# Output projection, norms and four feed-forward tiles in two column halves; three gate tiles first in the merge

## The chip, the cores and the metric

One core of a Trainium2 chip runs the whole program. The metric is the device time of one execution in microseconds (us); lower is better. The engines are named PE (TensorE, matrix products), ACT (ScalarE), DVE (VectorE), POOL (GpSimd) and SP (SyncE, which issues the transfers).

## The reference

One layer of a hybrid encoder for 512 prompt positions and 32 sample positions. What matters here comes after the two mixer branches (a Mamba-2 branch `y_ssm` and an attention branch `y_att`):

```python
merged = g_ssm * (y_ssm @ p['w_ssm_out']) + g_att * (y_att @ p['w_att_out'])
x = x + g1 * rmsnorm(merged @ p['w_out'], p['norm_mix_post'])
hn = rmsnorm(x, p['norm_ffn_pre']) * (1 + sc2) + sh2
gate, up = jnp.split(hn @ p['w_ffn_in'], 2, axis=-1)
gate, ffn_new = causal_dwconv(gate, ffn_ctx, p['ffn_conv_w'], p['ffn_conv_b'])
f = (jax.nn.silu(gate) * up) @ p['w_ffn_out']
x = x + g2 * rmsnorm(f, p['norm_ffn_post'])
```

The gates are sigmoids of columns of the input projection. Before `y_ssm` is multiplied, it is normalised in eight groups of 256 channels. D_MODEL is 1024, D_FF is 2816; all data are fp32.

## The kernel before

Activations lie with channels on the 128 partitions and positions in the columns: 512 prompt positions, a gap of 4 and 32 sample positions, TW = 548 columns, in two halves of HW = 274. A weight tile is 1024 input channels by 128 output channels, eight blocks of 128 x 128. For exactness each operand is split into a rounded part and a rest (`hi`, `lo`), and a product takes three matmuls per block and half: 48 matmuls of 274 columns for a tile. The result of a tile needs both halves, so two banks of PSUM, a "slot"; there are four slots.

**The weight stream** (class `Stream`). SP loads tile n into one of three raw buffers; ACT rounds it (`split_hi`), POOL subtracts (`split_lo`), PE multiplies (`multiply`) and counts `used`. There are two buffers for split weights, so `split_hi(n)` waits until tile n-2 is used up. The order of all waits and instructions is written out by hand for each engine, and each engine works strictly through its own list.

**The merge** (first block after the scan). PE computes the tile of the last gate, eight attention tiles (`w_att`), and then, for each of eight output tiles, a gate tile and two tiles of `w_ssm`: 33 tiles. Beside the attention tiles, the eight y groups are normalised: `load_y(g)` into one of `Y_SLOTS = 4` buffers `yl`, ACT's `square`, DVE's `add_squares`, PE's `sum_squares` (a product with ones), ACT's `y_root`, DVE's reciprocal and scaling, ACT's `y_hi` and POOL's `y_lo`. `load_y(g)` for g of 4 and more waits until `y_lo(g-4)` is done with the buffer. DVE's `gated(m)` evicts attention tile m; PE waits for `gated(m-2)` before it starts tile m. Attention data come in eight pieces through four buffers `al`. Before, ACT's round m of these runs as follows, and POOL's loop is the same in both kernels:

```python
for m in range(GROUPS + 1):          # ACT
    if m + 1 < GROUPS:
        square(m + 1)
        y_root(m + 1)
    if m >= 1:
        y_hi(m - 1)
    if m < GROUPS:
        w.split_hi(act, A0 + m + 2)
for m in range(GROUPS + 1):          # POOL
    w.split_lo(pool, A0 + m + 2)
    if m >= 1:
        y_lo(m - 1)
```

**Output projection and norms** (second block). Eight tiles of `w_out` over both halves; ACT copies each out of PSUM and squares it, DVE adds the squares, and after the last tile PE sums them over the channels. Then come the root, the reciprocal, the residual (DVE, eight tiles), the squares of the new x, root and reciprocal, the modulation (DVE), rounding (ACT) and rest (POOL). PE meanwhile makes four rows of the modulation vectors (`modulation_step`, `turn_rows`) and then the first feed-forward tile, block by block as `hq_lo` comes.

**Feed-forward** (third and fourth block). 44 tiles of `w_ffn_in`, in pairs gate and up, and 22 tiles of `w_ffn_out` in eight output tiles; the last norm ends the kernel. All blocks end with all engines waiting for one another.

Of the kernel before, what the change touches and what calls it, by code (L numbers as in the profile page):

```python
# [78 lines left out]
def build_layer(nc, i, o, scratch):  # L79
# [9 lines left out]
    with top:  # L89
# [21 lines left out]
        class Stream:  # L111
# [4 lines left out]
            def __init__(self, stack, tag, sources, base, ready, following):  # L116
# [5 lines left out]
                self.block = 0  # L122

# [3 lines left out]
            def hl_slot(self, n):  # L127
                return (self.base + n) % HL_SLOTS
# [19 lines left out]
            def split_hi(self, act, n):  # L148
# [4 lines left out]
                if n >= HL_SLOTS:  # L153
                    act.wait_ge(self.used, n - HL_SLOTS + 1)  # L154
# [17 lines left out]
            def multiply(self, pe, out, hi, lo, first, last, done=None):  # L172
# [1232 lines left out]
        with ExitStack() as st:  # L1405

            G1, A0 = 0, 1
# [9 lines left out]
            w = Stream(st, "m", src, NCH + GROUPS * GT + 1, True, [])  # L1417
            tmp = [sb(st, f"tmp{n}", [P, TW]) for n in range(3)]
# [7 lines left out]
            with ExitStack() as ms:  # L1426
# [14 lines left out]
                def sum_slot(g):  # L1441
                    return slot(3 - g % 2)

                with nc.Block(no_gpsimd_drain=True) as block:
                    @block.sync
                    def _(sp):
                        def load_y(g):
                            sp.dma_start(flat(yl[g % Y_SLOTS]), scratch["y"][g * P:(g + 1) * P, :]).then_inc(in_y[g % Y_SLOTS], 16)

                        load_y(0)  # L1450
                        for t in range(KB):
                            if t >= 4:
                                sp.wait_ge(alo_s, t - 3)
                            sp.dma_start(al[t % 4], scratch["att"][:, t, :]).then_inc(in_att[t % 4], 16)
                            if t == 3:
                                load_y(1)
                                sp.dma_start(snorm[:], i["ssm_norm"]).then_inc(in_c, 16)
                                w.load(sp, RAW_SLOTS)
                                load_y(2)
                        w.load(sp, RAW_SLOTS + 1)  # L1460
                        sp.wait_ge(alo_s, KB)
                        load_y(3)
                        w.load(sp, RAW_SLOTS + 2)
# [9 lines left out]
                    def _(pool):  # L1473
# [16 lines left out]
                    def _(act):  # L1490
# [17 lines left out]

                        w.split_hi(act, A0)
                        square(0)  # L1510
                        for t in range(KB):
# [15 lines left out]
                        for n in range(23):  # L1527
                            w.split_hi(act, N1 + n + 2)
                            if n % 3 == 0:
                                act.wait_ge(w.used, N1 + n + 1)  # L1530
                                act.wait_ge(m_s, KB + n // 3)
                                act.activation(halves(th[:]), slot(2), ACT.Tanh, scale=0.5).then_inc(th_s, 1)
# [8 lines left out]
                    def _(dve):  # L1541
# [8 lines left out]
                        def gated(m):  # L1550
# [4 lines left out]
                            dve.scalar_tensor_tensor(out=halves(mrg[:, m, :]), in0=halves(mrg[:, m, :]), scalar=1.0, in1=slot(m % 2),  # L1555
                                                     op0=ALU.add, op1=ALU.mult).then_inc(m_s, 1)

                        add_squares(0)
                        for t in range(KB):
                            dve.wait_ge(ahi_s, t + 1)  # L1560
                            dve.tensor_tensor(hq_lo[:, t, :], al[t % 4], hq_hi[:, t, :].bitcast(F32), ALU.subtract).then_inc(alo_s, 1)
                        dve.wait_ge(in_c, 16)
                        for m in range(KB):
                            if m >= 1:
                                gated(m - 1)
                            if m + 1 < GROUPS:
                                add_squares(m + 1)
                            dve.wait_ge(root_s, m + 1)
                            dve.reciprocal(rs[:, m % 2, :], rs[:, m % 2, :]).then_inc(rec_s, 1)
                            dve.wait_ge(rec_s, m + 1)  # L1570
# [619 lines left out]
```

## Time and profile before

| | us |
|---|---|
| median of 3 runs | 1434.98 |
| lowest, highest | 1433.67, 1438.44 |
| the profiled execution | 1436.78 |
| its span, first to last instruction | 1435.0 |

All numbers of the profile belong to the profiled execution. PE is the engine that works longest; its mean granted clock over the span was 0.959 of full speed. A matmul's end is modelled, so the distance between starts tells what one costs, and a busy PE may still be a slow one.

### The profile page before, as it was taken

Reading aid. Unit: us, or ns where it says so; the run is one execution under the profiler, and the core shown is the slowest. Engines: PE = TensorE matmul, PEld = TensorE weight load, DVE = VectorE, ACT = ScalarE, POOL = GpSimd, SP = SyncE. Lnnn points to the kernel's source line nnn. Section 1 sums busy time; section 2 is a strip of 40 time slices with the busy share of each in tenths; the row PEclk is TensorE's granted clock in tenths of the full one; section 3 lists DMA queues with packets and bytes.
Section 4 is the critical chain, followed back from the end, with each engine's and each line's share of the span. In section 5 each row is a group of like instructions: output and inputs, shape, how many; then the busy total and the mean of one; then the engine's idle time right before and its main releaser. Section 6 shows DMA issues by size and latency. Waiting matters only on the chain. (4 is left out here: it accounts for less than half of the span.)

```text
span 1435.0 us, 24802 instructions
## 1 busy us (share of the span) xinstructions
PE 1339.5 (93%) x10265; PEld 1255.5 (87%) x10265; DVE 809.9 (56%) x1288; ACT 508.1 (35%) x879; POOL 530.9 (37%) x315
## 2 busy tenths in 40 slices
PE   4699998999999999998798999988999999999996
PEld 1489988899899999998788999974899999999996
DVE  1745316898898898894780000337466666660105
ACT  2212425455455455453441222332332233332221
POOL 0533322332332333332464443332344444443443
PEclk8699989999999999999899999998799999999998
DMA  8275414433433433334331222541222222222221
GB/s 364 99 265 134 122 53 140 126 95 117 138 102 117 129 112 116 117 100 170 101 106 59 88 89 89 205 187 40 75 89 89 88 84 83 87 90 88 82 81 63
DMA packets 74015, 164.31 MB, mean 115 GB/s; under 512 B 28240, under 2 KB 42352, under 8 KB 70432
## 3 DMA queue, kind: packets, MB, share of 16 engines
q1 hardware_dynamic: 73904, 162.74, 35.2%
q8 instruction: 81, 1.33, 0.4%
q14 instruction: 30, 0.25, 0.1%
HBM read 147.10 MB, written 16.07 MB: 114 GB/s over the span
## 5 line engine op out<-in xcount | busy, mean ns | idle before, releaser
L161 POOL TENSOR_TENSOR w_lo<-raw_w,w_hi 128x1024 fp32r<-128x1024 f32 x174 | 429.0, 2466 | 730.3 <-ACT w_hi L155 730.3
L183 PE MATMUL psum<-hp_hi,w_hi 128*128 128x274 f32 x1472 | 449.8, 306 | 22.4 <-POOL hp_lo L284 13.4
L183 PE MATMUL psum<-hp_lo,w_hi 128*128 128x274 f32 x1472 | 430.9, 293 | 0.0
L183 PE MATMUL psum<-hp_hi,w_lo 128*128 128x274 f32 x1472 | 430.2, 292 | 0.0
L155 ACT ACTIVATE w_hi<-raw_w 128x1024 fp32r<-128x1024 f32 x174 | 184.1, 1058 | 547.0 <-PE psum L183 502.1
L183 PEld LDWEIGHTS psum<-hp_hi,w_hi 128*128 128x128 f32 x1472 | 281.7, 191 | 36.5 <-POOL hp_lo L284 16.1
L183 PEld LDWEIGHTS psum<-hp_lo,w_hi 128*128 128x128 f32 x1472 | 284.5, 193 | 1.3
L183 PEld LDWEIGHTS psum<-hp_hi,w_lo 128*128 128x128 f32 x1472 | 282.7, 192 | 0.0
L183 PE MATMUL psum<-hq_hi,w_hi 128*128 128x274 f32 x832 | 248.7, 299 | 12.5 <-POOL hq_lo L1677 8.5
L183 PE MATMUL psum<-hq_hi,w_lo 128*128 128x274 f32 x832 | 245.5, 295 | 0.0
L183 PE MATMUL psum<-hq_lo,w_hi 128*128 128x274 f32 x832 | 244.2, 294 | 0.0
L183 PEld LDWEIGHTS psum<-hq_hi,w_hi 128*128 128x128 f32 x832 | 161.3, 194 | 16.3 <-POOL hq_lo L1677 11.6
L183 PEld LDWEIGHTS psum<-hq_lo,w_hi 128*128 128x128 f32 x832 | 162.4, 195 | 0.4
L183 PEld LDWEIGHTS psum<-hq_hi,w_lo 128*128 128x128 f32 x832 | 160.8, 193 | 0.0
L1096 DVE SCALAR_TENSOR_TENSOR cv<-raw,gp_all,cv 128x548 f32<-128x548 f32 x96 | 93.1, 976 | 14.2 <-ACT cv L978 12.2
L183 PE MATMUL psum<-y_hi,w_hi 128*128 128x274 f32 x256 | 75.4, 295 | 6.2 <-POOL y_lo L1477 6.2
L1588 DVE SCALAR_TENSOR_TENSOR tmp<-th,psum 128x548 f32<-128x548 f32 x8 | 5.8, 723 | 126.2 <-PE psum L183 126.2
L183 PE MATMUL psum<-y_lo,w_hi 128*128 128x274 f32 x256 | 75.1, 293 | 0.0
L183 PE MATMUL psum<-y_hi,w_lo 128*128 128x274 f32 x256 | 75.0, 293 | 0.0
L1891 DVE COPY fr<-fpar 128x2 f32<-128x2 f32 x22 | 41.2, 1874 | 58.9 <-ACT fr L1866 58.9
L1902 DVE SCALAR_TENSOR_TENSOR fs<-th,tmp 128x548 f32<-128x548 f32 x22 | 53.0, 2408 | 32.1 <-ACT th L1873 32.1
L1123 DVE TENSOR_SCALAR dec<-acs_b,tok_all 128x128 f32<-128x128 f32 (+1 forms) x160 | 66.1, 473 | 8.4 <-PE psum L1272 8.4
(263 smaller groups left out, 2033.0 us busy)
## 6 DMA issues: line engine op xcount, KB each, us to landing
raw_w<-in_w_grp SPq DMA_DIRECT2D x58, 512.0 KB, 3.8
raw_w<-in_w_ffn_in SPq DMA_DIRECT2D x44, 512.0 KB, 3.6
ada<-in_w_ada SPq DMA_DIRECT2D x12, 1024.0 KB, 20.6
raw_w<-in_w_ffn_out SPq DMA_DIRECT2D x22, 512.0 KB, 3.5
acs_b<-mem_acs SPq DMA_DIRECT2D x8, 1096.0 KB, 5.6
raw_w<-in_w_ssm SPq DMA_DIRECT2D x16, 512.0 KB, 3.5
ada_o<-in_w_ada SPq DMA_DIRECT2D x4, 2048.0 KB, 11.3
raw_w<-in_w_qkv SPq DMA_DIRECT2D x13, 512.0 KB, 4.9
```

The lines of the kernel that those rows point to most:

```text
L155: act.activation(flat(w_hi[self.hl_slot(n)]), raw_w[self.raw_slot(n)][:], ACT.Copy).then_inc(self.hi_done, 1)
L161: eng.tensor_tensor(flat(w_lo[self.hl_slot(n)]), raw_w[self.raw_slot(n)][:], flat(w_hi[self.hl_slot(n)]).bitcast(F32), ALU.subtract).then_ ...
L183: mm = pe.matmul(out[:, h, :], w, x[:, cols], start=first and j == 0, stop=last and j == 2)
L1096: ins = dve.scalar_tensor_tensor(out=cv[:, t, :], in0=raw[:, t, 1 + k:1 + k + TW], scalar=par(g, GP_W + 4 * t + k, GP_W + 4 * t + k + 1), ...
L1123: ins = dve.tensor_scalar(dec[u % 2][0:L, r, 0:L], acs_b[0:L, r, c0:c0 + L], tok_all[0:L, g, c, 2, r:r + 1], 0.0, ALU.add, ALU.min)
L1588: link(dve, dve.scalar_tensor_tensor(out=halves(tmp[0][:]), in0=halves(th[:]), scalar=1.0, in1=slot(m % 2), op0=ALU.add, op1=ALU.mult))
L1891: link(dve, dve.tensor_copy(r[:, LEAD + S0 - 2:LEAD + S0], fpar[:, f, 4:6]))
L1902: dve.scalar_tensor_tensor(out=sl[f % 2][:], in0=th[:], scalar=1.0, in1=c[:], op0=ALU.add, op1=ALU.mult).then_inc(fsl_s, 1)
```

## The change

**Merge.** Three gate tiles (the last, the first and the second) come ahead of the attention tiles, and so each SSM pair is followed by the gate tile of two pairs on. The attention data are loaded through four other buffers, and the roundings, squares and roots are put into a new order: in ACT's loop the squares of group m+3 and the root of group m+2 now belong to round m. POOL takes two of the attention rests.

**Two halves.** The output projection runs first over the left half of the columns for all eight weight tiles, then over the right half. The split weights stay on chip for that: to the two buffers come six more (`w.plan` says which tile goes where, `w.wait_free` what it must wait for; `half` multiplies one half). While PE works on the right half, the other engines take the left half through both norms; then PE takes the left half of the first four feed-forward tiles, while the right half goes through the norms, and last the right half of those tiles. The modulation rows are spread between the tiles; that of the last gate is turned only in the last block (`turn_s`).

**Feed-forward.** It starts at tile 4. Weights take turns in four buffers instead of two (`split_ahead`), and the extra pair for the very last weight goes.

The stream: what a split waits for, and the product of one half.

```diff
-if n >= HL_SLOTS:
+if n in self.wait_free:
+    sem, count = self.wait_free[n]
+    if count:
+        act.wait_ge(sem, count)
+elif n >= HL_SLOTS:
     act.wait_ge(self.used, n - HL_SLOTS + 1)
...
+def half(self, pe, out, n, k, hi, lo, h, done=None):
+    if k == 0:
+        self.wait_split(pe, n)
+    wh, wl = w_hi[self.hl_slot(n)][:, k, :], w_lo[self.hl_slot(n)][:, k, :]
+    for j, (w, x) in enumerate(((wh, hi), (wh, lo), (wl, hi))):
+        mm = pe.matmul(out, w, x[:, k, h * HW:(h + 1) * HW], start=k == 0 and j == 0, stop=k == KB - 1 and j == 2)
+    if k == KB - 1 and done is not None:
         mm.then_inc(done, 1)
```

The order of the merge's tiles, and the plan of the split weights (`first` and `second` are the two old buffers).

```diff
-src = [i["w_gate"][8 + KB - 1]] + [i["w_att"][m] for m in range(KB)]
+src = [i["w_gate"][8 + KB - 1], i["w_gate"][0], i["w_gate"][1]] + [i["w_att"][m] for m in range(KB)]
 for m in range(KB):
-    src += [i["w_gate"][m], i["w_ssm"][2 * m], i["w_ssm"][2 * m + 1]]
+    src += [i["w_ssm"][2 * m], i["w_ssm"][2 * m + 1]]
+    if m + 2 < KB:
+        src.append(i["w_gate"][m + 2])
...
+SECOND_PASS = (2, 3, 4, 5, 0, 1, 6, 7)
+w.plan.update({O0: first, O0 + 1: second, O0 + 6: 2, O0 + 7: 3})
+for n in range(4):
+    w.plan[O0 + 2 + n] = w.plan[F0 + n] = 4 + n
+for n in range(F0 + 4, END):
+    w.plan[n] = (first, second, 2, 3)[(n - F0) % 4]
+    w.wait_free[n] = (w.used, n - 3)
+for n in range(2, KB):
+    w.wait_free[O0 + n] = (None, 0)
+for n in range(KB):
+    w.wait_free[F0 + n] = (free_s, n + 1)
```

ACT in the merge.

```diff
+w.split_hi(act, 1)
+square(0)
+att_hi(0)
+act.wait_ge(w.used, G1 + 1)
+act.activation(halves(mrg[:, KB - 1, :]), slot(0), ACT.Tanh, scale=0.5).then_inc(ev_s, 1)
+w.split_hi(act, 2)
+y_root(0)
+square(1)
+for t in range(1, 4):
+    att_hi(t)
 w.split_hi(act, A0)
-square(0)
-for t in range(KB):
-    if t == KB - 2:
-        act.wait_ge(w.used, G1 + 1)
-        act.activation(halves(mrg[:, KB - 1, :]), slot(2), ACT.Tanh, scale=0.5).then_inc(ev_s, 1)
-    act.wait_ge(in_att[t % 4], 16 * (t // 4 + 1))
-    act.activation(hq_hi[:, t, :], al[t % 4], ACT.Copy).then_inc(ahi_s, 1)
+gate_tanh(0, 1, slot(1))
+att_hi(4)
+att_hi(5)
 w.split_hi(act, A0 + 1)
-y_root(0)
+gate_tanh(1, 2, slot(0))
+att_hi(6)
+att_hi(7)
+y_root(1)
+square(2)
 for m in range(GROUPS + 1):
-    if m + 1 < GROUPS:
-        square(m + 1)
-        y_root(m + 1)
     if m >= 1:
         y_hi(m - 1)
     if m < GROUPS:
         w.split_hi(act, A0 + m + 2)
-for n in range(23):
+    if m + 2 < GROUPS:
+        y_root(m + 2)
+    if m + 3 < GROUPS:
+        square(m + 3)
+for n in range(21):
     w.split_hi(act, N1 + n + 2)
```

DVE in the merge, its second part.

```diff
+att_lo(6)
+att_lo(7)
+y_reciprocal(1)
+y_norm(1)
+add_squares(2)
+add_squares(3)
+for g in range(2, GROUPS):
+    y_reciprocal(g)
+    if g + 2 < GROUPS:
+        add_squares(g + 2)
+    gated(g - 2)
+    y_norm(g)
+gated(KB - 2)
 gated(KB - 1)
```

PE in the merge: gate tiles and attention tiles; then the SSM tiles and the first two half tiles of the output projection.

```diff
+tile(0, hp_hi, hp_lo)
+tile(1, hp_hi, hp_lo, 0, 2)
+pe.wait_ge(ev_s, 1)
+tile(0, hp_hi, hp_lo, 1, 4)
 for m in range(KB):
-    if m >= 2:
+    if m < 2:
+        pe.wait_ge(th_s, m + 1)
+    else:
         pe.wait_ge(m_s, m - 1)
     for k in range(KB):
         if m == 0:
-            pe.wait_ge(alo_s, k + 1)
-        w.multiply(pe, slot(m % 2), hq_hi[:, k, :], hq_lo[:, k, :], k == 0, k == KB - 1)
-        if k == 4 and m + 1 < GROUPS:
-            sum_squares(m + 1)
-pe.wait_ge(root_s, GROUPS)
+            wait_att_lo(pe, k)
+        w.multiply(pe, att_slot(m), hq_hi[:, k, :], hq_lo[:, k, :], k == 0, k == KB - 1)
+        if k == 3 and m + 2 < GROUPS:
+            sum_squares(m + 2)
 for m in range(KB):
...
-tile(m % 2, wide_hi, wide_lo, 0, 16)
-tile(m % 2, wide_hi, wide_lo, 8, 16)
...
+    for k in range(16):
+        if m == 0:
+            pe.wait_ge(ylo_s, k + 1)
+        w.multiply(pe, slot(m % 2), wide_hi[:, k, :], wide_lo[:, k, :], k == 0, k == 15)
+    if m + 2 < KB:
+        if m == 0:
+            pe.wait_ge(root_s, GROUPS)
+        else:
+            pe.wait_ge(th_s, m + 2)
+        tile(2, hp_hi, hp_lo)
 for k in range(KB):
     pe.wait_ge(mlo_s, k + 1)
-    w.multiply(pe, slot(0), hp_hi[:, k, :], hp_lo[:, k, :], k == 0, k == KB - 1)
...
+    w.half(pe, psum[:, 0, 0:HW], O0, k, hp_hi, hp_lo, 0, w.used)
+for k in range(KB):
+    w.half(pe, psum[:, 2, 0:HW], O0 + 1, k, hp_hi, hp_lo, 0, w.used)
```

ACT's eviction of a half tile of the output projection; c counts the left half's eight tiles, then the right half's.

```diff
+def out_tile(c):
+    h, j = divmod(c, KB)
+    t = SECOND_PASS[j] if h else j
+    bank = 2 * (j % 2) + h
+    if h:
+        act.wait_ge(free_s, j + 1)
+    else:
+        act.wait_ge(w.used, O0 + j + 1)
+    if c >= 2:
+        act.wait_ge(add_s, 7 * h + j - 2 if j >= 3 else 7 * h + 1 if j == 2 else 6 + j)
+    act.activation(sqo[c % 2], psum[:, bank, 0:HW], ACT.Square).then_inc(sqo_s, 1)
+    act.activation(half_of(mrg[:, t, :], h), psum[:, bank, 0:HW], ACT.Copy).then_inc(ev_s, 1)
```

ACT's order from the end of the left half on.

```diff
+row(0)
+out_root(0)
+w.split_hi(act, F0)
+out_tile(8)
+square(0)
+square(1)
+w.split_hi(act, F0 + 1)
+out_tile(9)
+square(2)
+square(3)
+square(4)
...
+w.split_hi(act, F0 + 2)
+out_tile(10)
+square(5)
+square(6)
+square(7)
+w.split_hi(act, F0 + 3)
+x_root(0)
+out_tile(11)
+h_hi(0)
+h_hi(1)
+out_tile(12)
+h_hi(2)
+h_hi(3)
+h_hi(4)
+out_tile(13)
+h_hi(5)
+h_hi(6)
+h_hi(7)
+out_tile(14)
+w.split_hi(act, F0 + 4)
+out_tile(15)
+out_root(1)
+w.split_hi(act, F0 + 5)
+for c in range(8, 12):
+    square(c)
```

PE in the second block: both passes of the output projection.

```diff
+for m in range(2, KB):
+    pe.wait_ge(ev_s, m - 1)
     for k in range(KB):
...
+        w.half(pe, psum[:, 2 * (m % 2), 0:HW], O0 + m, k, hp_hi, hp_lo, 0, w.used)
+    if m >= 6:
+        row_steps(m - 6)
+mid = {0: (3, lambda: out_squares(0)), 2: (3, lambda: x_squares(1)), 3: (3, lambda: x_squares(4)),
+       4: (3, lambda: x_squares(7))}
+for j, m in enumerate(SECOND_PASS):
+    if j >= 2:
+        pe.wait_ge(ev_s, KB + j - 1)
+    for k in range(KB):
+        w.half(pe, psum[:, 2 * (j % 2) + 1, 0:HW], O0 + m, k, hp_hi, hp_lo, 1, free_s)
+        if j in mid and mid[j][0] == k:
+            mid[j][1]()
+    if j < 2:
+        row_steps(2 + j)
+    if j == 1:
+        x_squares(0)
+    elif j == 2:
+        pe.wait_ge(ev_s, KB)
+        for a in range(2):
+            pe.wait_ge(row_s, a + 1)
+            mm = turn_rows(pe, 0, 8 * a, mod_row[:, a, :])
+        mm.then_inc(turn_s, 1)
+        x_squares(2)
+        x_squares(3)
+    elif j == 3:
+        x_squares(5)
+        x_squares(6)
```

PE in the second block: four feed-forward tiles, left halves, then right halves.

```diff
+for n in range(4):
+    for k in range(KB):
+        if n == 0:
+            pe.wait_ge(hlo_s, k + 1)
+        w.half(pe, psum[:, ffn_bank(n), 0:HW], F0 + n, k, hq_hi, hq_lo, 0)
+        if n == 0 and k == 4:
+            out_squares(1)
+    if n == 1:
+        pe.wait_ge(ev_s, 2 * KB)
+        row_steps(4)
+        row_steps(5)
+        x_squares(8)
+        x_squares(9)
+    elif n == 2:
+        for c in range(10, 16):
+            x_squares(c)
+        row_steps(6)
+        row_steps(7)
+pe.wait_ge(row_s, 4)
 for k in range(KB):
...
+    pe.wait_ge(hlo_s, KB + k + 1)
+    for n in range(3):
+        w.half(pe, psum[:, ffn_bank(n) + 1, 0:HW], F0 + n, k, hq_hi, hq_lo, 1, w.used)
 for k in range(KB):
...
+    w.half(pe, psum[:, ffn_bank(3) + 1, 0:HW], F0 + 3, k, hq_hi, hq_lo, 1, w.used)
+w.block = (F0 + 4) * KB
```

Splits ahead in the feed-forward block; n counts its tiles.

```diff
+def split_ahead(split, eng, n):
+    if n < 2:
+        split(eng, F0 + 6 + n)
+    elif n >= 5:
+        split(eng, F0 + n + 3)
```

Left out are the SP order, the declarations and DVE's order in the second block: sums of the left half's squares (`add_out`), reciprocal, the left half's eight `residual`, reciprocal and eight `modulated`, with the right half's `add_out` put in between as its tiles come, and then the same for the right half. `residual` and `modulated` are the operations of before on one half.

## Rows read from the trace of the kernel before

**Rows 1.** The page, part 1: PE's busy time, share of span, instructions.

```profile
PE 1339.5 (93%) x10265; PEld 1255.5 (87%) x10265; DVE 809.9 (56%) x1288; ACT 508.1 (35%) x879; POOL 530.9 (37%) x315
```

**Rows 2.** Busy time by stretch (windows): stretch, length, engines' busy us, PEclk, DMA.

```profile
667.96:763.75 95.79, 75.11 (x513) 71.22 (x513) 63.12 (x48) 43.46 (x55) 50.91 (x27) 0.92 0.41 136
763.75:906.43 142.68, 142.68 (x1105) 142.68 (x1105) 14.32 (x18) 30.80 (x36) 54.47 (x22) 0.98 0.25 78
906.43:957.40 50.97, 49.47 (x386) 48.82 (x384) 16.25 (x13) 17.38 (x23) 19.80 (x8) 1.00 0.67 265
957.40:1017.83 60.43, 45.36 (x180) 26.32 (x181) 39.68 (x55) 17.57 (x26) 14.96 (x11) 0.75 0.09 24
1017.83:1038.00 20.17, 20.17 (x146) 20.17 (x147) 10.37 (x12) 6.71 (x8) 8.02 (x7) 0.91 0.41 129
```

**Rows 3.** Timeline of PE in the merge: start, us, instruction [idle before <-releaser].

```profile
688.03 2.19 PE L1610 MATMUL psum<-tmp,ones 128*128 128x274 f32 x4 [5.40 <-DVE tmp L1548]
...
698.35 1.19 PE L1610 MATMUL psum<-tmp,ones 128*128 128x274 f32 x4 [0.43 <-DVE tmp L1548]
...
699.51 0.29 PE L183 MATMUL psum<-hq_lo,w_hi 128*128 128x274 f32 x1
...
763.75 0.60 PE L183 MATMUL psum<-y_hi,w_hi 128*128 128x274 f32 x1 [6.21 <-POOL y_lo L1477]
```

**Rows 4.** Timeline of ACT in the merge.

```profile
681.45 0.61 ACT L1514 ACTIVATE mrg<-psum 128x548 f32<-128x548 f32 x1
...
684.12 1.28 ACT L1501 ACT_TABLE_LOAD   x1
685.41 0.72 ACT L1501 ACTIVATE y_rstd<-psum,consts 128x548 f32<-128x548 f32 x1
...
701.92 1.06 ACT L155 ACTIVATE w_hi<-raw_w 128x1024 fp32r<-128x1024 f32 x1 [0.52 <-PE psum L183]
...
712.41 1.12 ACT L1495 ACTIVATE ysq<-yl 128x1096 f32<-128x1096 f32 x1 [1.56 <-DMA yl<-mem_y]
```

**Rows 5.** Timeline of POOL ahead of the first SSM tile.

```profile
758.76 2.34 POOL L161 TENSOR_TENSOR w_lo<-raw_w,w_hi 128x1024 fp32r<-128x1024 f32 x1 [1.05 <-ACT w_hi L155]
761.06 2.63 POOL L1477 TENSOR_TENSOR y_lo<-yl,y_hi 128x548 fp32r<-128x548 f32 x2
```

**Rows 6.** Transfers in the merge: engine, count, KB each, median us to landing.

```profile
yl<-mem_y SPq DMA_DIRECT2D x8, 548.0 KB, 3.6
```

**Rows 7.** Timeline of DVE in the merge.

```profile
706.09 3.56 DVE L1569 RECIPROCAL y_rstd<-y_rstd 128x548 f32<-128x548 f32 x1
709.69 1.49 DVE L1573 SCALAR_TENSOR_TENSOR yl<-yl,snorm,y_rstd 128x548 f32<-128x548 f32 x2
711.10 0.72 DVE L1555 SCALAR_TENSOR_TENSOR mrg<-mrg,psum 128x548 f32<-128x548 f32 x1
713.57 1.78 DVE L1548 TENSOR_TENSOR tmp<-ysq 128x548 f32<-128x548 f32 x1 [1.75 <-ACT ysq L1495]
```

**Rows 8.** Timeline of PE at the output projection's first tile and block end.

```profile
912.98 0.39 PE L183 MATMUL psum<-hp_hi,w_hi 128*128 128x274 f32 x1 [1.05 <-DVE hp_lo L1579]
...
914.45 0.36 PE L183 MATMUL psum<-hp_hi,w_hi 128*128 128x274 f32 x1 [0.45 <-PEq L1444]
```

**Rows 9.** Timeline of PE: turning two rows, then steps of two rows.

```profile
985.85 1.84 PE L210 MATMUL psum<-pick_rows,mod_row_o 128*128 128x2 f32 x16
987.62 3.64 PE L203 MATMUL psum<-ada_o,c_silu 128*32 128x512 f32 x32
```

**Rows 10.** Timeline of DVE in the norms: residual tiles, then modulation tiles.

```profile
974.06 0.72 DVE L1734 TENSOR_TENSOR mrg<-mrg,ors 128x548 f32<-128x548 f32 x1
...
975.65 0.72 DVE L1734 TENSOR_TENSOR mrg<-mrg,ors 128x548 f32<-128x548 f32 x1
...
999.80 0.71 DVE L1751 TENSOR_TENSOR tmp<-mrg,ors 128x548 f32<-128x548 f32 x1
...
1002.25 0.72 DVE L1751 TENSOR_TENSOR tmp<-mrg,ors 128x548 f32<-128x548 f32 x1
```

More of the change, by code:

```diff
@@ L1562, in _, with att_lo @@
[L1562 to L1574 removed]
+                        def att_lo(t):
+                            dve.wait_ge(ahi_s, t + 1)
+                            dve.tensor_tensor(hq_lo[:, t, :], al[t], hq_hi[:, t, :].bitcast(F32), ALU.subtract).then_inc(alo_s, 1)
@@ L1691, in _ @@
-                        for n in range(KB):
-                            if n < KB - 1:
-                                w.split_hi(act, O0 + n + 2)
-                            act.wait_ge(w.used, O0 + n + 1)
-                            act.activation(halves(mrg[:, n, :]), slot(n % 2), ACT.Copy).then_inc(ev_s, 1)
-                            act.wait_ge(ev_s, n + 1)
-                            square(n, n)
-                        w.split_hi(act, F0 + 1)
-                        act.wait_ge(ss_s, 1)
@@ new lines, in _ @@
+                        for m in range(KB):
+                            if m + 2 < KB:
+                                w.split_hi(act, O0 + m + 2)
+                            out_tile(m)
+                        row(0)
[7 more added lines that the diff above has]
+                        square(2)
@@ L1718, in _ @@
                         row(2)
+                        for c in range(12, 16):
+                            square(c)
+                        x_root(1)
                         row(3)
+                        for c in range(8, 16):
+                            h_hi(c)
                     @block.vector
@@ L1744, in _ @@
+                        for c in range(1, KB):
+                            add_out(c)
+                        reciprocal(1, O_BANK[0], 0)
+                        for t in range(3):
+                            residual(t)
+                        add_out(9)
+                        for t in range(3, 6):
+                            residual(t)
+                        add_out(10)
+                        residual(6)
+                        residual(7)
                         dve.wait_ge(turn_s, 1)
-                        link(dve, add_bias(dve, 4 * KB, KB, 6))
+                        link(dve, add_bias(dve, 4 * KB, KB, 0))
@@ new lines, in _ @@
+                        add_out(12)
+                        modulated(5)
+                        modulated(6)
+                        modulated(7)
+                        add_out(13)
+                        add_out(14)
+                        add_out(15)
+                        reciprocal(3, O_BANK[1], 1)
+                        for c in range(8, 16):
+                            residual(c)
+                        reciprocal(4, X_BANK[1], 1)
+                        for c in range(8, 16):
+                            modulated(c)
@@ L1761, in _ @@
                     @block.tensor
                     def _(pe):
-                        def squares(src, s, first, last):
-                            for hh in range(2):
-                                mm = pe.matmul(psum[:, 2 * s + hh, 0:HW], ones[:], src[:, hh * HW:(hh + 1) * HW],
-                                               start=first, stop=last)
-                            mm.then_inc(ss_s, 1)
-                        for m in range(1, KB):
-                            if m >= 2:
-                                pe.wait_ge(ev_s, m - 1)
-                            for k in range(KB):
-                                w.multiply(pe, slot(m % 2), hp_hi[:, k, :], hp_lo[:, k, :], k == 0, k == KB - 1)
@@ L1792, in _, with sums @@
-                        pe.wait_ge(ev_s, KB)
-                        for k in range(KB):
-                            block_step(0, k)
-                        for t in range(KB):
-                            block_step(1, t)
-                            pe.wait_ge(sq_s, KB + t + 1)
-                            squares(sq[t % 2], 2, t == 0, t == KB - 1)
-                        pe.wait_ge(root_s, 1)
-                        turn(0, 6)
-                        for a in (2, 3):
-                            for k in range(KB):
-                                block_step(a, k)
+                        def sums(bank, src, first, last):
+                            return pe.matmul(psum[:, bank, 0:HW], ones[:], src, start=first, stop=last)
```

405 lines of the change are left out of this document (248 added, 157 removed).

## The prediction

> **What bounds the kernel now.** I read the page first: TensorE (PE) is busy for 93% of the span [rows 1], so only time in which PE stands still or runs at a lower granted clock can be won. Then the stretches around the change [rows 2]. The second one, 763.75 to 906.43, holds 23 weight tiles (eight SSM pairs, seven gate tiles) at a granted clock of 0.98; less the 2.9 us that the missing 2% is worth this is 139.8/23 = **6.08 us a tile** at full clock (the upper of the two levels, 2.4 GHz), 3.04 for half the columns. The first stretch holds 10 tiles (60.8 us) in 95.79 us, so the start of the merge loses some 35 us less the sums. The fourth, where the norms sit, holds a single tile in 60.43 us, at a clock of 0.75. The change works on these two.
>
> PE's own timeline in the merge [rows 3] shows three things. Sums of squares for one group cost 1.03 us (698.35 to 699.51, less one 0.13 us matmul). Small waits for DVE stand in front of them. And at 763.75 PE waits 6.21 us for `y_lo`. The reader should look at that one closely: in POOL's queue [rows 5] `y_lo` of the last group stands behind a weight split (`w_lo`), which waits for ACT's `split_hi`, which waits until PE has finished a tile. From the tile's end to `y_lo` done it takes 6.2 us, however early the y data were ready.
>
> **The change part by part.** The sum is made against the profiled execution, 1436.78 us around a span of 1435.0, 0.13% above the median.
>
> *Merge.* The work is the same: 33 tiles (200.6) and eight sums (8.2), 208.8 us. Before, the merge lasted from 667.96 to 906.43, 238.5 us, so 29.7 are waits and clock. After:
>
> (a) Three gate tiles come first (18.2 us, two sums in them) and cover the attention loads and the first reciprocal: the 5.40 us wait [rows 3] goes. At attention tile 0, step 3, the new order wants the sums of group 2. They stand behind, from the end of the third gate tile: ACT's split 1.06, tanh 0.61, two roundings of 0.6, table load 1.28, root 0.72 [rows 4]; DVE's reciprocal 3.56, two scalings 1.49, one add (0.72 like its neighbour of that width, 1.78 beside POOL) [rows 7]: 10.9 us with hops, while PE arrives after 3.04. Wait 7.9. At tile 1 split, root, square and add take 3.7 to 4.7 us against 3.04: 0.9.
>
> (b) The squares of group m+3 are now taken in ACT's round m; before it was group m+1. There are four `yl` buffers, so from group 4 on the load needs `y_lo` of group m-1, and POOL does that in the same round m, behind the split for attention tile m+2 that waits for the end of tile m. That is the queue of rows 5, moved from one place to four (m = 1 to 4). ACT stands at the square until the load is there; DVE stands at `add_squares(m+3)`, and behind it in DVE's queue is `gated(m-1)`, which PE awaits before attention tile m+1. Nothing else is issued to PE in between. The price: 6.21 to `y_lo` [rows 3, 5], load 3.6 [rows 6], square 1.12 [rows 4], add 0.72, `gated` 0.72 [rows 7], hops 0.2: **12.6 us, four times: 50.4**. Lower bound 12.3 (no hops, the load at its median); upper 15 (add 1.78, and the load slowed by the next weight behind it, 1.4).
>
> (c) The 6.21 us wait before the first SSM tile goes: its y parts are awaited one by one. In its place `gated(7)` (0.85) and the last `y_lo`, again behind a split (0.8): 1.6.
>
> (d) Clock: the 6.21 us wait left PE at half clock afterwards, worth the 2.9 us above. Five waits of 7.9 to 12.6 us at 2.7 each: 13.5. Below: 1.0 each, if it recovers sooner.
>
> Merge after: 208.8 + 7.9 + 0.9 + 50.4 + 1.6 + 13.5 = 283.1; **+44.6 us**.
>
> *Output projection to the fourth feed-forward tile.* Before: 906.43 to 1038.00, 131.6 us [rows 2]. After, from the same start:
> - First half tile: step 7 needs the last `hp_lo`, which came at 912.98 [rows 8], 6.55 us after the first matmul; a half tile gets there in 2.7, so the wait grows from 1.05 to 3.9. Then 27 matmuls, 3.4, and 1.5 for clock: 11.5.
> - The next weight's split can begin only in the new block: barrier 0.6 (0.45 idle beyond a modelled end [rows 8]), split 1.06 + 2.34 [rows 4, 5]: 4.1. Before, full tiles gave it cover.
> - Six half tiles 18.2, two row steps (3.64/4 = 0.9 each [rows 9]), clock 2.7, weights late behind the modulation blocks 1: 23.7.
> - Second pass: eight half tiles 24.3, two row steps 1.8, eight half sums 4.0, one more 0.5, turning rows 1.84 [rows 9], and 1.3 where ACT's written order holds an eviction back: 33.7. Under it run the residual (1.59 a tile at full width, 0.8 to 0.95 at half) and the modulation of the first half (2.45, so 1.23) [rows 10]. From the first sum on: root 1.7 with its table, reciprocal 1.8, eight residuals 7.6, adds 1.2, root and reciprocal 2.2, eight modulations 9.8, hops and waits for sums about 9, together some 33 us: they just fit. This is the cover that pays; each us that it is short is lost.
> - First halves of four feed-forward tiles 12.2, row steps 3.6, sums 4.5, waits for the second half's residual 2.5: 22.8.
> - Second halves: after the last sum the chain is root 0.4, reciprocal 1.8, eight modulations 9.8, rounding 1.2, last step 1.1 and the fourth tile's 3.04, less 4.9 of PE work that lies beside it: 12.5.
> - New block: barrier 0.6, split 1.06 and eviction 0.61 before tile 4 can start; the first SiLU chain, formerly under three tiles, has one to hide in: 1.0; clock 1.5: 4.8.
>
> Sum 113.1; **-18.5 us**. Bounds: -28 (no clock loss, no small waits) and 0 (chains at full-width prices). The turned rows of the last gate move into the last block, +1.84 with no cover. Keeping the last weight in four slots instead of an extra pair: nothing; its split has a whole tile of 16.7 us as cover, and 3.4 if that were gone. The steady feed-forward tiles are at PE's pace before and stay so.
>
> Total: 1436.8 + 44.6 - 18.5 + 1.8 = 1464.7 in the profiled execution; less 1.8, **1463 us** as a median, 2.0% slower.
>
> **Rivals.** *The reloads of y are hidden* (other side, faster). Before, the square waits only 1.56 us for its load [rows 4] and the adds cost PE about half a us. It decides if `y_lo(m-1)` is done before tile m ends; then 4 x (12.6 - 0.8) and four clock losses of 2.7 go: 1463 - 58 = 1405. Against it stands the order of POOL's queue, which the 6.21 us wait shows at work.
>
> *The halves give nothing back.* Half-width operations may keep much of their full price on DVE and ACT (fixed cost, POOL beside them); the two norms then take as long as before, and the stage stays at 131.6: 1463 + 18.5 = 1482. For it: of the modulation's 2.45 us only 0.72 are its multiplication [rows 10]; the rest is dearer than DVE's other operations of that width [rows 7], with POOL at work beside it. Against: PE has twelve half tiles of other work.
>
> *The clock stays low in the four tiles.* Between waits of 12.6 us PE works for 7; if all of that ran at the lower level (1.2 GHz) each tile would lose another 3.4: 1477. Against: after 5.40 us of waiting the sums at 698.35 already ran at full price, after one tile [rows 3].
> The Trainium skill, page "TensorE: Matmul & The Clock Gate", section "HAM oscillation", tells of a kernel that waits for data once in every tile and starts every tile slow; by that rule this rival is the likely one, and the rows above bear out the slow start but not a slow whole tile.
>
> *The halves give far more*: with no wait left PE needs for that stage twelve tiles (73.0), row steps 7.3, sums 9 and turning 1.84, some 91 us; then 40 us are won instead of 18.5: 1441.
>
> **How the numbers follow.** Chances: forecast 0.80, y hidden 0.08, halves give nothing 0.05, low clock 0.04, halves give far more 0.03. A measurement of this kernel tells about 0.3% (4.3 us) from no change. Faster is the first rival, 0.08; same the part of the last in which the merge is cheaper too, 0.03; slower the rest, 0.89. The forecast's own range: low 1463 - 1 (b at 12.3) - 8 (clock) - 10 (stage) = 1444; high + 10 (b at 15) + 15 (stage) = 1488. With the last rival taken in it is 1441 to 1488; three rivals lie inside, the first and the unforeseen, about 2 in 10, outside.
>
> **What would show it.** Right: between the third gate tile and the SSM tiles, one PE wait near 8 us released by DVE's sum, then four of 12 to 13 us before attention tiles 2 to 5, released by `gated`; ACT's square waiting for `yl`; the merge some 283 us; first output-projection matmul to feed-forward tile 4 some 113 us. Wrong: no such four waits (then (b) has failed), or a stage that is not near 113 (then a chain of the halves was mis-sized). The steady feed-forward should not move.

## The result, and the profile after

The changed kernel takes **1469.42 us** (median of four, 1467.98 to 1471.41) against 1436.45 us of the kernel before (median of four, the three of the table above and one more): ratio 1.0232, 95% interval 1.0208 to 1.0256. It is 2.3% slower. The forecast was 1463 us, slower, in a range of 1441 to 1488.

First the busy times by stretch in the changed kernel: the merge up to the first SSM tile, the SSM and gate tiles, the output projection and norms up to feed-forward tile 4, and the rest. The fields are as in [rows 2].

```profile
core 0: us, PE busy (x) PEld busy (x) DVE busy (x) ACT busy (x) POOL busy (x), PEclk, DMA share, GB/s
666.98:813.89 146.91, 85.51 (x561) 82.17 (x561) 60.69 (x46) 43.98 (x56) 45.83 (x25) 0.79 0.26 89
813.89:949.50 135.61, 134.92 (x1057) 134.48 (x1058) 14.32 (x18) 32.01 (x38) 59.69 (x26) 1.00 0.27 82
949.50:1063.26 113.76, 98.69 (x695) 87.17 (x693) 71.68 (x107) 43.97 (x90) 45.38 (x32) 0.97 0.44 160
1063.26:1467.00 403.74, 386.61 (x3000) 385.04 (x3000) 177.46 (x203) 113.39 (x147) 176.19 (x112) 0.98 0.26 81
```

The merge grew from 238.5 us [rows 2] to 282.5 us (146.91 + 135.61), and all of that is in the first line, where PE is busy for only 85.51 of 146.91 us (it holds eleven tiles, one more than the first stretch of [rows 2]). The norms' stage shrank from 131.6 to 113.8 us. The timeline of PE in the merge, only rows in front of which PE stood still, with the idle time in brackets:

```profile
start us, us, engine line op out<-in xcount [idle before <-releaser]
699.64 2.19 PE L1714 MATMUL psum<-tmp,ones 128*128 128x274 f32 x4 [9.24 <-DVE tmp L1635]
...
709.84 1.19 PE L1714 MATMUL psum<-tmp,ones 128*128 128x274 f32 x4 [1.23 <-DVE tmp L1635]
...
726.40 0.60 PE L188 MATMUL psum<-hq_hi,w_hi 128*128 128x274 f32 x1 [12.30 <-DVE mrg L1642]
...
748.18 0.59 PE L188 MATMUL psum<-hq_hi,w_hi 128*128 128x274 f32 x1 [12.63 <-DVE mrg L1642]
...
769.30 0.59 PE L188 MATMUL psum<-hq_hi,w_hi 128*128 128x274 f32 x1 [12.56 <-DVE mrg L1642]
...
791.66 0.60 PE L188 MATMUL psum<-hq_hi,w_hi 128*128 128x274 f32 x1 [12.55 <-DVE mrg L1642]
```

Where [rows 3] had one wait of 5.40 and one of 6.21 us, there are now one of 9.24 and four of 12.3 to 12.6, all four released by `gated` (L1642). Such a line names only the last releaser. To see what `gated` waited for, one round is followed through the other queues, in the timelines of ACT, POOL, SyncE's queue and DVE. Tile 1 of the attention ends at 726.40 - 12.30 = 714.10. ACT first:

```profile
714.20 1.06 ACT L160 ACTIVATE w_hi<-raw_w 128x1024 fp32r<-128x1024 f32 x1 [4.75 <-PE psum L188]
715.16 0.70 ACT L1568 ACTIVATE y_rstd<-psum,consts 128x548 f32<-128x548 f32 x1
723.83 1.12 ACT L1560 ACTIVATE ysq<-yl 128x1096 f32<-128x1096 f32 x1 [7.97 <-DMA yl<-mem_y]
```

POOL in the same round:

```profile
715.33 2.34 POOL L166 TENSOR_TENSOR w_lo<-raw_w,w_hi 128x1024 fp32r<-128x1024 f32 x1 [6.13 <-ACT w_hi L160]
717.63 2.63 POOL L1535 TENSOR_TENSOR y_lo<-yl,y_hi 128x548 fp32r<-128x548 f32 x2
```

SyncE's queue, the reload of y:

```profile
720.29 0.33 SPq L1497 DMA_DIRECT2D yl<-mem_y  x1
```

DVE, the add and `gated`:

```profile
724.98 0.73 DVE L1635 TENSOR_TENSOR tmp<-ysq 128x548 f32<-128x548 f32 x1 [11.71 <-ACT ysq L1560]
725.63 0.72 DVE L1642 SCALAR_TENSOR_TENSOR mrg<-mrg,psum 128x548 f32<-128x548 f32 x1
```

The telling row is POOL's first: before the split it stood idle for 6.13 us, waiting for the end of the tile, with `y_lo` behind it in the queue; the run `y_lo` first below shows that `y_lo` could have run in that time. Only when `y_lo` is done (720.26) is the reload issued (720.29); it is there at 723.8, and then the square, the add and `gated` follow one after the other. This is the chain of the prediction's part (b), link by link.

### The profile page after: what moved, and what is told of

Read it like the earlier page. It is cut to its first block and busy times, and to the rows that moved or that the text cites. A ratio compares the mean times of both kernels' runs of the same rounds, so it can differ in the third digit from the quotient of the medians.

```text
span 1467.0 us, 24927 instructions
## 1 busy us (share of the span) xinstructions
PE 1329.5 (91%) x10265; PEld 1252.8 (85%) x10265; DVE 793.6 (54%) x1327; ACT 514.7 (35%) x915; POOL 540.8 (37%) x325
## 5 line engine op out<-in xcount | busy, mean ns | idle before, releaser
L166 POOL TENSOR_TENSOR w_lo<-raw_w,w_hi 128x1024 fp32r<-128x1024 f32 x135 | 335.6, 2487 | 614.1 <-ACT w_hi L160 614.1
L188 PE MATMUL psum<-hp_hi,w_hi 128*128 128x274 f32 x1292 | 397.8, 308 | 19.7 <-POOL hp_lo L299 12.7
L188 PE MATMUL psum<-hq_hi,w_hi 128*128 128x274 f32 x448 | 136.8, 305 | 54.7 <-DVE mrg L1642 50.0
L188 PE MATMUL psum<-hq_hi,w_lo 128*128 128x274 f32 x448 | 133.8, 299 | 0.0
L188 PE MATMUL psum<-hq_lo,w_hi 128*128 128x274 f32 x448 | 133.4, 298 | 0.0
L166 POOL TENSOR_TENSOR wx_lo<-raw_w,wx_hi 128x1024 fp32r<-128x1024 f32 x32 | 76.9, 2405 | 108.0 <-ACT wx_hi L160 108.0
L188 PE MATMUL psum<-hq_hi,wx_lo 128*128 128x274 f32 x320 | 92.7, 290 | 0.0
L188 PE MATMUL psum<-hq_hi,wx_hi 128*128 128x274 f32 x320 | 92.7, 290 | 0.0
L188 PE MATMUL psum<-hq_lo,wx_hi 128*128 128x274 f32 x320 | 92.6, 289 | 0.0
L188 PEld LDWEIGHTS psum<-hq_lo,w_hi 128*128 128x128 f32 x448 | 89.5, 200 | 0.3
L188 PEld LDWEIGHTS psum<-hq_hi,w_lo 128*128 128x128 f32 x448 | 88.5, 198 | 0.0
```

The costliest lines, as they stand in the source:

```text
L166: eng.tensor_tensor(flat(w_lo[self.hl_slot(n)]), raw_w[self.raw_slot(n)][:], flat(w_hi[self.hl_slot(n)]).bitcast(F32), ALU.subtract).then_ ...
L188: mm = pe.matmul(out[:, h, :], w, x[:, cols], start=first and j == 0, stop=last and j == 2)
```

## The experiments

The ratios are to the kernel before, run on the same chip. A merge length is the time from the first merge matmul to the first matmul of the output projection in the profiled execution (282.5 in the changed kernel, 238.5 before). The part ahead of the merge is not touched by these edits, yet it took between 663.1 and 669.3 us in the nine profiles, so the stretches say more than a difference of a few us in the totals.

| kernel | ratio, 95% interval | merge | stage to tile 4 |
|---|---|---|---|
| changed | 1.0232, 1.0208 to 1.0256 | 282.5 | 113.8 |
| `y_lo` first | 1.0030, 1.0016 to 1.0044 | 250.2 | 118.7 |
| `gated` first | 1.0173, 1.0147 to 1.0200 | 271.3 | 118.4 |
| both | 0.9940, 0.9916 to 0.9964 | 236.3 | 115.7 |
| halves only | 0.9943, 0.9919 to 0.9966 | 238.2 | 116.3 |
| waits filled | 1.0209, 1.0176 to 1.0241 | 274.3 | 118.5 |
| all orders | 0.9835, 0.9808 to 0.9863 | 221.6 | 116.0 |
| last step late | 0.9804, 0.9777 to 0.9831 | 220.1 | 113.7 |

Theory T is that of the prediction: the order of POOL's queue makes the reload late. Its rivals are D (the order on DVE alone) and M (four y buffers are too few, the transfer sets the pace).

**`y_lo` first.** One line moves in POOL's program:

```diff
 for m in range(GROUPS + 1):
-    w.split_lo(pool, A0 + m + 2)
     if m >= 1:
         y_lo(m - 1)
+    w.split_lo(pool, A0 + m + 2)
```

> In POOL's queue of the merge, y_lo of group m-1 is put ahead of the split for attention tile m+2; nothing else of the changed kernel is touched. Theory T (the queue order makes the reload late): the reload is landed when tile m ends, and each of the four waits before attention tiles 2 to 5 shrinks from 12.5 us to split 1.06 + root 0.70 + square 1.12 + add 0.73 + gated 0.72 = 4.3 us. Four times 8.2 us go, and about 1 us of low clock with each: 1469 - 37 = 1432 us (1426 to 1442). Rival D (the order on VectorE alone, gated behind the add, holds PE): the load is not what it waits for, waits stay at 12.5 us, 1469 us. Rival M (four y buffers are too few, and the transfer itself sets the pace): only POOL's split of 2.34 us leaves the chain, 4 x 2.3 us, 1460 us.

Measured: 1437.49 us, 2.0% less than the changed kernel by the ratios; the merge lost 32.3 us. PE's waits in this kernel's merge (total, times, longest):

```profile
PE psum L188 <- DVE mrg L1642: 20.3, 5, 4.9
PE psum L1714 <- DVE tmp L1635: 10.4, 2, 9.2
```

Its ACT timeline in one round:

```profile
710.13 1.06 ACT L160 ACTIVATE w_hi<-raw_w 128x1024 fp32r<-128x1024 f32 x1 [4.76 <-PE psum L188]
711.09 0.70 ACT L1568 ACTIVATE y_rstd<-psum,consts 128x548 f32<-128x548 f32 x1
712.07 1.12 ACT L1560 ACTIVATE ysq<-yl 128x1096 f32<-128x1096 f32 x1 [0.28 <-DMA yl<-mem_y]
```

Its POOL timeline, with `y_lo` now ahead of the split:

```profile
705.09 3.21 POOL L1535 TENSOR_TENSOR y_lo<-yl,y_hi 128x548 fp32r<-128x548 f32 x2
711.26 2.35 POOL L166 TENSOR_TENSOR w_lo<-raw_w,w_hi 128x1024 fp32r<-128x1024 f32 x1 [2.96 <-ACT w_hi L160]
```

And its DVE timeline:

```profile
713.22 0.97 DVE L1635 TENSOR_TENSOR tmp<-ysq 128x548 f32<-128x548 f32 x1 [4.00 <-ACT ysq L1560]
714.12 0.71 DVE L1642 SCALAR_TENSOR_TENSOR mrg<-mrg,psum 128x548 f32<-128x548 f32 x1
```

ACT's wait for the load fell from 7.97 to 0.28 us: the transfer fits under a tile, so M is out, and D too, since the waits fell with DVE's order as it was. The four waits are 4.85 us, 0.5 more than expected: the add took 0.97 beside POOL's split instead of 0.73, and the load still came 0.28 late.

**`gated` first.** In DVE's round `gated(g - 2)` goes ahead of `add_squares(g + 2)`:

```diff
 y_reciprocal(g)
+gated(g - 2)
 if g + 2 < GROUPS:
     add_squares(g + 2)
-gated(g - 2)
 y_norm(g)
```

> On VectorE, gated(g-2) is put ahead of add_squares(g+2) in the merge; POOL's order stays as in the changed kernel. Theory T: the chain through the reload stays as long as it was and only its last step leaves it; the wait moves from the start of attention tiles 2 to 5 to the sum behind their step 3, and is shorter by gated 0.72 and four steps of 0.76 us, so about 8.8 us instead of 12.5. Four times 3.7 us: 1469 - 15 = 1454 us (1450 to 1460). Rival D (the order on VectorE alone): the waits vanish, four times 12.5 us and the low clock behind them, 1469 - 58 = 1411 us. Rival M: as T.

Measured: 1457.49 us. The waits moved to the sums as T has it, from the same view of PE:

```profile
723.89 2.20 PE L1714 MATMUL psum<-tmp,ones 128*128 128x274 f32 x4 [8.57 <-DVE tmp L1635]
...
743.02 2.19 PE L1714 MATMUL psum<-tmp,ones 128*128 128x274 f32 x4 [9.01 <-DVE tmp L1635]
```

8.6 to 9.0 us where 8.8 was expected. As long as the reload is late, DVE's order is worth its last link and the four steps, no more; D is out a second time.

**Both edits.**

> Both edits together: y_lo ahead of the split on POOL, gated ahead of the add on VectorE. Theory T: the chain behind a tile's end is split 1.06 + root 0.70 + square 1.12 + add 0.73 = 3.6 us, and PE has four steps of 3.04 us to do meanwhile, so the four waits are 0.6 us each; 4 x 11.9 us and 4 x 2 us of low clock go: 1469 - 56 = 1413 us (1407 to 1424), 1.6% faster than the kernel before. Rival M (the transfer sets the pace): some 5 us of each wait stay, 1469 - 30 = 1439 us. If the gain is that of the first edit alone, rival D's part is nothing.

Measured: 1424.25 us, 0.6% faster than before where T gave 1.6%, just beyond the slow edge of its range. The merge is 236.3, so 46.2 went; but the waits did not all fall to 0.6 us. PE's timeline in this kernel:

```profile
714.49 1.19 PE L1714 MATMUL psum<-tmp,ones 128*128 128x274 f32 x4 [1.14 <-DVE tmp L1635]
...
722.21 0.39 PE L188 MATMUL psum<-hq_hi,w_hi 128*128 128x274 f32 x1 [3.47 <-DVE mrg L1642]
```

DVE's timeline ahead of the second of these:

```profile
714.36 3.73 DVE L1657 SCALAR_TENSOR_TENSOR yl<-yl,snorm,y_rstd 128x548 f32<-128x548 f32 x2
718.01 3.56 DVE L1651 RECIPROCAL y_rstd<-y_rstd 128x548 f32<-128x548 f32 x1
721.50 0.66 DVE L1642 SCALAR_TENSOR_TENSOR mrg<-mrg,psum 128x548 f32<-128x548 f32 x1
```

I had overlooked that the reciprocal (3.56 us) also stands ahead of `gated`; once the reload was early, DVE's own queue became the longest chain in every second round (3.47 us each time, 1.1 us in the rounds between). The two scalings took 3.73 us here, against 1.48 in the changed kernel, with POOL at `y_lo` at the same time (713.99, 3.52 us). The Trainium skill, page "SBUF — State Buffer", section "Who interferes with whom", says that a VectorE instruction with two inputs from SBUF contends with a GpSimd instruction that reads SBUF; the trace agrees: the scalings read `yl` and `y_rstd` and are slowed, and `gated`, which has an input in PSUM, took 0.66 us beside POOL's split (719.98, 2.35 us).

**Halves only.** The merge of the kernel before, with its own order of weights, and behind it the new stage unchanged.

```diff
-G1, A0 = 0, 3
-src = [i["w_gate"][8 + KB - 1], i["w_gate"][0], i["w_gate"][1]] + [i["w_att"][m] for m in range(KB)]
+G1, A0 = 0, 1
+src = [i["w_gate"][8 + KB - 1]] + [i["w_att"][m] for m in range(KB)]
 for m in range(KB):
-    src += [i["w_ssm"][2 * m], i["w_ssm"][2 * m + 1]]
-    if m + 2 < KB:
-        src.append(i["w_gate"][m + 2])
+    src += [i["w_gate"][m], i["w_ssm"][2 * m], i["w_ssm"][2 * m + 1]]
...
```

> The merge in the order of the kernel before (one gate tile, eight attention tiles, then gate and SSM tiles), and behind it the output projection, norms and first feed-forward tiles in two halves as in the changed kernel. Theory T (the two parts add up): 1469 less the merge's 44 us, 1425 us (1420 to 1430), 0.8% faster than the kernel before. Rival (the gain of the halves comes from the state in which the new merge leaves the queues, with weights and turned rows in place): the stage is longer than 114 us, and the time is that of the kernel before or above, 1436 us or more.

Measured: 1424.46 us. Its stretches (merge, stage, rest):

```profile
669.34:907.50 238.16, 217.73 (x1616) 213.85 (x1617) 78.69 (x66) 74.16 (x91) 105.30 (x49) 0.96 0.31 102
907.50:1023.80 116.30, 102.17 (x695) 90.61 (x693) 70.68 (x107) 44.31 (x90) 45.32 (x32) 0.93 0.42 156
1023.80:1427.60 403.80, 386.64 (x3000) 385.07 (x3000) 177.60 (x203) 113.44 (x147) 176.26 (x112) 0.98 0.26 81
```

The parts add up: the halves give back 15.3 us here (131.6 to 116.3) as against 17.8 in the changed kernel, and cost 6.8 behind (403.8 against 397.0). The stage is 2.5 us longer than in the changed kernel, as the rival had it, but the time is not: PE's long waits in it have the same lengths, and the granted clock is 0.93 instead of 0.97.

**Waits filled.** PE does useless matmuls in its five long waits; nobody reads them.

```diff
+def fill(g, count):
+    pe.wait_ge(root_s, g - 1)
+    for j in range(count):
+        pe.matmul(sum_slot(g)[:, j % 2, :], hq_hi[:, 0, 0:P], hq_hi[:, 0, 0:HW], start=True, stop=True)
...
+if m == 0:
+    fill(2, 70)
 sum_squares(m + 2)
...
+if m < 6:
+    fill(m + 2, 94)
 pe.wait_ge(m_s, m - 1)
```

> The changed kernel with PE kept at work in its five long waits of the merge: 70 extra matmuls of 0.13 us ahead of the sum in attention tile 0, and 94 each ahead of attention tiles 2 to 5, into a sum bank that is free there; nobody reads them. No other engine's order changes, so the chains through the reload keep their length. What the prediction charged to the clock in (d), 13.5 us, is tested by itself. If it is the clock: PE is at the upper level behind each wait, 1469 - 8 to 13 us, 1456 to 1461 us. If the tiles behind the waits are slow for another reason (the loads beside them, or a wait that the records don't show): 1469 us or a little above, since the filling ends at best with the wait.

Measured: 1463.2 us; the interval of the ratio overlaps that of the changed kernel, so the total alone decides nothing. The merge does. Its stretches up to the first SSM tile, that of the SSM tiles, and the stage:

```profile
663.38:802.02 138.64, 133.53 (x1006) 130.49 (x1007) 60.73 (x46) 43.95 (x56) 46.44 (x25) 1.00 0.28 95
802.02:937.64 135.62, 134.93 (x1057) 134.49 (x1058) 14.33 (x18) 32.00 (x38) 59.69 (x26) 1.00 0.25 82
937.64:1056.10 118.46, 104.28 (x695) 92.18 (x693) 71.03 (x107) 44.19 (x90) 45.31 (x32) 0.91 0.41 153
```

The granted clock of the first is 1.00 instead of 0.79, and it is 8.3 us shorter though PE had 446 more matmuls to do: that much was clock. 4.7 us of it were lost again in the stage, by two drops of the clock that the changed kernel's profile did not have (last section); by this profile that is why the total is above the 1456 to 1461 us.

**All orders.** On top of both edits, DVE's round becomes `gated`, reciprocal, scalings, add, and the chain to the sums of group 2 is taken off the end of the third gate tile (ACT's lines below; DVE's add of group 2 and the load of the second attention weight move ahead likewise):

```diff
 att_hi(5)
+y_root(1)
+square(2)
 w.split_hi(act, A0 + 1)
-gate_tanh(1, 2, slot(0))
 att_hi(6)
 att_hi(7)
-y_root(1)
-square(2)
+gate_tanh(1, 2, slot(0))
```

> On top of both edits: VectorE's round is gated, reciprocal, two scalings, add (with the reciprocal ahead of gated, that kernel still waited 3.47 us for gated once); and ahead of attention tile 0, the root of group 1 and the square of group 2 are taken on ScalarE before the split that waits for the third gate tile, the tanh behind the last two roundings, the add of group 2 before the last two differences, and the load of the second attention weight is issued two loads earlier. Theory T: the wait of 9.2 us at attention tile 0 goes to 0 to 2 us, the ones of 1.2 and 3.5 to about 1, with some 3 us of low clock: 1424 - 14 = 1410 us (1403 to 1418), 1.6% faster than the kernel before. If the loads of the attention rows, not the order of the queues, hold that tile: the wait stays at 5 us or more and the time at 1418 us or above.

Measured: 1410.36 us, 1.65% faster than before. The 9.24 us wait is gone; PE's timeline, the first rows with a wait in front (three more of 1.2 us follow in the attention tiles):

```profile
687.06 1.19 PE L1714 MATMUL psum<-tmp,ones 128*128 128x274 f32 x4 [0.29 <-DVE tmp L1635]
...
690.30 0.40 PE L188 MATMUL psum<-hq_hi,w_hi 128*128 128x274 f32 x1 [0.52 <-DVE hq_lo L1647]
...
697.69 1.19 PE L1714 MATMUL psum<-tmp,ones 128*128 128x274 f32 x4 [2.56 <-DVE tmp L1635]
...
707.71 1.19 PE L1714 MATMUL psum<-tmp,ones 128*128 128x274 f32 x4 [1.23 <-DVE tmp L1635]
```

The merge is 221.6 us, 16.9 less than before. With the queues in this order, the merge that begins with three gate tiles beats the old one, which the order of the queues had hidden.

**Last step late.** The first half tile's last step behind seven steps of the second:

```diff
-for k in range(KB):
-    pe.wait_ge(mlo_s, k + 1)
-    w.half(pe, psum[:, 0, 0:HW], O0, k, hp_hi, hp_lo, 0, w.used)
-for k in range(KB):
-    w.half(pe, psum[:, 2, 0:HW], O0 + 1, k, hp_hi, hp_lo, 0, w.used)
+for n, bank, k0, k1 in ((0, 0, 0, KB - 1), (1, 2, 0, KB - 1), (0, 0, KB - 1, KB), (1, 2, KB - 1, KB)):
+    for k in range(k0, k1):
+        pe.wait_ge(mlo_s, k + 1)
+        if n == 1 and k == 0:
+            pe.wait_ge(m_s, 2 * KB)
+        w.half(pe, psum[:, bank, 0:HW], O0 + n, k, hp_hi, hp_lo, 0, w.used)
```

> As the kernel with all orders changed, and at the start of the output projection the last step of the first half tile, which waits 3.7 us for the last hp_lo, is put behind seven steps of the second half tile. The wait that the prediction priced at 3.9 is then under 2.66 us of work, less the wait for the last SSM merge that now stands ahead of the second tile: 1 to 2.5 us less than that kernel, some 1408 us. If the split of the third weight, which comes behind both tiles, is later bound by something else than their end: no difference.

Measured: 1405.21 us. The wait of 3.67 us there became one of 2.19, and the stage is 113.7. The difference to the kernel with all orders is about 0.3%, with overlapping intervals, and not all of it is the edit: the merge, which the edit leaves alone, is 1.5 us shorter too. From the first matmul of the stage to the third weight it took 12.7 us instead of 16.6: 1.5 is the shorter wait, 2.4 is less busy time of PE for the same matmuls, at a granted clock of 1.00 instead of 0.76. Whether the shorter wait kept the clock up there was not tested. As a whole this kernel beats both kernels of this case, by 2.0% and 4.2%.

## Why the prediction was right, and where its terms were off

The mechanism of (b) carried the slowdown, and it was the right one: mending POOL's order alone took back 2.0 of the 2.3%. There were four waits where they were said to be, released by `gated`, behind ACT's square that waits for `yl`. The profiled execution was forecast at 1464.7 us and took 1468.85: the merge came 0.6 us under its forecast, the stage 3.2 and what lies behind it 2.4 over, and the part ahead of the merge was 1.0 shorter than before. What each term came to:

- **(a)** 7.9 forecast, 9.24 measured, because ACT's split there waited 3.46 us for its weight (`raw_w<-in_w_att`) and began at 689.04, 1.8 us behind the end of the third gate tile (687.2); I had not followed that load through SyncE's queue. From the split on the chain took 10.6 us, where 10.9 was forecast. Tile 1: 0.9 forecast, 1.23.
- **(b)** 50.4 forecast; 12.30 + 12.63 + 12.56 + 12.55 = 50.0. The bounds of 12.3 and 15 a wait were not needed.
- **(c)** 1.6 forecast; `gated` 0.89 and two `y_lo` of 0.41 and 0.28 make 1.6.
- **(d)** the term that was mis-sized: 13.5 forecast. From a wait's end to the next wait's start the changed kernel takes 9.15 us in tile 2 (726.40 to 735.55), and with the waits filled 7.13 (721.50 to 728.63): 2.0 us. In the same way 1.7 (tile 0), 1.4, 2.7 and 1.7 for the others, 9.5 in all. That is 1.9 a wait, where 2.7 was taken. The 2.9 us of the one wait before [rows 2] came from a clock rounded to 0.98; over 763.75 to 770 it is 0.60, which is 2.5 us.

The merge was 282.5 where 283.1 was forecast, because (d)'s 4.0 too many met (a)'s 1.7 too few and some 2 us more; that the total is so close is luck. Of the 2 us the tile price gives 1.7: the 22 tiles of the second stretch kept PE busy for 134.92 us at a clock of 1.00, 6.13 us a tile and not 6.08, and there are 33.

- **The stage.** 113.8 up to tile 4, where the pieces up to there gave 110.6. The rows of PE in it:

```profile
955.99 0.59 PE L200 MATMUL psum<-hp_hi,w_hi 128*128 128x274 f32 x1 [3.67 <-DVE hp_lo L1685]
...
965.17 0.36 PE L200 MATMUL psum<-hp_hi,wt_hi 128*128 128x274 f32 x1 [4.04 <-POOL wt_lo L166]
...
1004.30 1.05 PE L225 MATMUL psum<-pick_rows,mod_row_o 128*128 128x2 f32 x8 [1.62 <-ACT mod_row_o L1881]
...
1024.66 0.28 PE L200 MATMUL psum<-hq_hi,wt_hi 128*128 128x274 f32 x1
...
1063.26 0.40 PE L188 MATMUL psum<-hq_hi,w_hi 128*128 128x274 f32 x1 [2.20 <-ACT fr L2161]
...
1072.05 0.60 PE L188 MATMUL psum<-hq_hi,w_hi 128*128 128x274 f32 x1 [2.43 <-DVE fs L2200]
```

  The first three pieces came as forecast: 11.6 (11.5), 4.04 (4.1), 23.6 (23.7; the second pass starts at 988.8). The second pass took 35.9 instead of 33.7: PE stands 1.62 us for ACT's copy of the second row, and another 0.75 for an eviction, 1.1 more than the 1.3 set aside; the other 1.1 is not separated. The first halves took 22.5, where 22.8 was forecast. The second halves took 13.9 instead of 12.5; 1.0 of that is the modulation, which costs 0.43 + 0.97 beside POOL, about 1.35 a tile, where half of [rows 10] gave 1.23.
- **Behind it.** 403.7 us against 397.0 before, 6.7 more; 1.8 + 2.5 were forecast. The SiLU chain left tile 5 waiting 2.43 us, not 1.0, and the turned rows took their 1.84; about 1 us is not assigned.

Of the rivals, *the reloads are hidden* is what the kernel does when POOL's order is mended: that was its own condition, and it came true only when it was made true. Its price was too good: without DVE's order mended as well, 4.85 us stay of each wait, not 0.8. *The clock stays low through whole tiles* did not happen: 1.4 to 2.7 us are lost behind a wait, not 2.7 + 3.4. The Trainium skill, page "TensorE: Matmul & The Clock Gate", section "HAM oscillation", tells of a kernel that waits for data ahead of every tile and starts every tile slow; the trace agrees: the first matmul behind each of the four waits took 0.59 to 0.60 us, and 0.39 us with the waits filled. *The halves give nothing back* falls with the halves-only kernel, and *the halves give far more* did not happen: PE still waits in the stage, as its rows above show.

## What to carry to other kernels

A queue runs in the order written: an instruction that waits for the end of a tile holds back all that stands behind it, however long ready. When an operation is taken two rounds earlier, follow the buffer that it reads back through every queue to what frees it, and put that ahead of anything that waits for the current tile. When one chain is cut, work out the second longest before promising its whole length: here DVE's reciprocal took over at once.

## What the runs showed that was not expected

The norms' stage has the same instructions in the seven kernels with the old order of steps, and yet took 113.8 to 118.7 us. Almost all of the difference lies in three places:

| from, to | changed | `y_lo` first | `gated` first | both | halves only | waits filled | all orders |
|---|---|---|---|---|---|---|---|
| first matmul, third weight | 15.7 | 15.7 | 15.7 | 15.8 | 16.8 | 15.7 | 16.6 |
| turned rows, next wait for an eviction | 15.7 | 18.9 | 18.9 | 17.3 | 17.3 | 18.9 | 17.3 |
| feed-forward halves, up to tile 4 | 36.5 | 38.0 | 38.1 | 36.5 | 36.6 | 38.1 | 36.5 |

Where a piece is longer, its granted clock is lower: 0.77 (halves only) and 0.76 (all orders) against 0.89 in the first row, 0.82 (`y_lo` first) against 1.00 in the second, 0.96 (`y_lo` first) against 1.00 in the third. The second row makes most of the difference. The stretch before the turned rows and that of the turned rows in the kernel with all orders:

```profile
920.00:935.00 15.00, 15.00 (x114) 11.28 (x107) 7.46 (x10) 7.04 (x14) 2.47 (x2) 1.00 0.20 56
935.00:946.00 11.00, 9.38 (x58) 8.65 (x57) 9.29 (x14) 4.53 (x12) 4.68 (x2) 0.84 0.47 151
```

The same two in the changed kernel:

```profile
985.00:1000.00 15.00, 15.00 (x113) 11.83 (x112) 7.93 (x9) 7.40 (x14) 3.58 (x2) 1.00 0.19 59
1000.00:1011.00 11.00, 9.38 (x67) 8.84 (x66) 8.49 (x14) 4.85 (x10) 3.60 (x2) 1.00 0.48 149
```

In both, PE was busy throughout the 15 us before, at full clock, then turned rows in matmuls of two columns and stood still for 1.62 us. In one the granted clock fell to a mean of 0.84, in the other it stayed at 1.00. Over such a stretch it was 0.69 to 0.84 in all seven experiments, and 1.00 in the changed kernel alone. Why it fell there and not here was not settled; a difference of up to 5 us between two profiles of this stage can be no more than this.
